# Two transformer blocks in one kernel: the joints between stages rearranged, conditioning rows on the ring's queue, a reordered last mixer

## The reference

```python
# first block; cs = silu(c)
for l in range(2):
    mod = cs @ ada_w[l] + ada_b[l]                       # 1024 x 6144
    sh1, sc1, g1, sh2, sc2, g2 = split(mod, 6)
    h = rms_norm(x, norm_mix_g[l]) * (1 + sc1) + sh1
    x = x + g1 * hybrid_mixer(h, w_in[l], w_out[l], ...)  # attention and retention
    h = rms_norm(x, norm_ffn_g[l]) * (1 + sc2) + sh2
    f = swiglu(h, ...) if l == 0 else moe_ffn(h, ...)     # dense FFN, then 8 experts, top 2
    x = x + g2 * f
x = rms_norm(x, final_norm_g)
# second block
for l in range(2):
    x = x + 0.5 * swiglu(rmsnorm(x, ffn1_norm[l]), ...)
    x = x + even_mixer(x) if l == 0 else x + odd_mixer(x)
    x = x + 0.5 * swiglu(rmsnorm(x, ffn2_norm[l]), ...)
```

## Time and profile before

| | |
|---|---|
| median of 3 runs | 2357.81 us (2356.74 to 2358.11) |
| profiled execution | 2357.99 us, span 2356.4 us |
| TensorE busy | 2257.9 us, 96% |
| VectorE busy | 1703.7 us, 72% |
| ScalarE busy | 1401.6 us, 59% |
| mean granted TensorE clock | 0.983 of full speed |
| moved by DMA | 571.54 MB, mean 243 GB/s |

### The profile page before, as it was taken

The page is one execution under the profiler, slowest core; times in us unless marked ns, Lnnn a source line. Parts: engine busy times, 40 slices in busy tenths (PEclk is TensorE's granted clock), DMA queues, the critical chain, the costliest instruction groups (busy, mean ns, idle before and its releaser), DMA issues.

```text
span 2356.4 us, 34524 instructions
## 1 busy us (share of the span) xinstructions
PE 2257.9 (96%) x10548; PEld 1865.6 (79%) x10548; DVE 1703.7 (72%) x2237; ACT 1401.6 (59%) x2059; POOL 27.8 (1%) x56
## 2 busy tenths in 40 slices
PE   7998998998999999999999899999999999879999
PEld 6877886787888888888887678877888888767887
DVE  5877777867989989999999855576555554754554
ACT  4545445556787787777777644465544544575443
POOL 0000110000000000000000000000000000000000
PEclk9999999998999999999999999999999999989999
DMA  9775885847999999999999765543656555412661
GB/s 374 271 223 193 306 296 177 303 137 205 362 349 367 352 349 367 348 367 355 355 360 351 269 196 180 195 152 118 199 183 194 171 184 172 151 45 68 210 196 54
DMA packets 403943, 571.54 MB, mean 243 GB/s; under 512 B 27868, under 2 KB 324376, under 8 KB 403832
## 3 DMA queue, kind: packets, MB, share of 16 engines
q1 hardware_dynamic: 394032, 543.13, 68.8%
q0 software_dynamic: 6304, 22.62, 3.0%
q10 hardware_dynamic: 3496, 4.39, 0.5%
HBM read 568.99 MB, written 1.05 MB: 242 GB/s over the span
## 4 chain that ended last, share of the span: by engine, by line
PE 84%; DVE 8%; ACT 5%; issue 3%; DMA 0%; ACTq 0%; DVEq 0%
PE bank L371 75%; DVE lo L350 3%; ACT hi L348 1%; PE bank L566 1%; PE bank L2668 1%; ACT xn L102 1%; DVE acc_sum L312 1%; PE bank L831 1%; PE bank L2795 1%; DVE small L102 1%; ACT aT_hi L102 1%; PE bank L2737 0%; PE bank L1862 0%; DVE rope_tmp L102 0%; DVE aT_lo L102 0%
## 5 line engine op out<-in xcount | busy, mean ns | idle before, releaser
L350 DVE TENSOR_TENSOR lo<-raw,hi 128x1024 fp32r<-128x1024 f32 x981 | 1158.8, 1222 | 180.8 <-ACT hi L348 167.1
L348 ACT ACTIVATE hi<-raw 128x1024 fp32r<-128x1024 f32 x981 | 987.7, 1054 | 95.6 <-PE bank L371 94.9
L371 PE MATMUL bank<-hi,aT_hi 128*128 128x512 f32 (+1 forms) x2016 | 812.7, 403 | 21.3 <-DVE aT_lo L102 8.5
L371 PE MATMUL bank<-hi,aT_lo 128*128 128x512 f32 (+1 forms) x2016 | 790.5, 392 | 0.0
L371 PE MATMUL bank<-lo,aT_hi 128*128 128x512 f32 (+1 forms) x2016 | 788.6, 391 | 0.0
L371 PEld LDWEIGHTS bank<-hi,aT_hi 128*128 128x128 f32 x2016 | 382.9, 190 | 104.3 <-issue 13.5
L371 PEld LDWEIGHTS bank<-hi,aT_lo 128*128 128x128 f32 x2016 | 381.7, 189 | 81.6
L371 PEld LDWEIGHTS bank<-lo,aT_hi 128*128 128x128 f32 x2016 | 383.2, 190 | 74.6 <-issue 1.7
L371 PE MATMUL bank<-hi,hidT_hi 128*128 128x512 f32 x792 | 310.1, 392 | 0.9 <-DVE hidT_lo L2676 0.9
L371 PE MATMUL bank<-hi,hidT_lo 128*128 128x512 f32 x792 | 308.4, 389 | 0.0
L371 PE MATMUL bank<-lo,hidT_hi 128*128 128x512 f32 x792 | 308.3, 389 | 0.0
(11 more groups left out here) (313 smaller groups left out, 1540.5 us busy)
## 6 DMA issues: line engine op xcount, KB each, us to landing
raw<-moe_w_gate SPq DMA_DIRECT2D x352, 256.0 KB
raw<-moe_w_up SPq DMA_DIRECT2D x352, 256.0 KB
raw<-moe_w_down SPq DMA_DIRECT2D x176, 512.0 KB
raw<-ffn_w_gu SPq DMA_DIRECT2D x352, 256.0 KB
raw<-ffn_w_down SPq DMA_DIRECT2D x110, 512.0 KB
raw<-ada_units SPq DMA_DIRECT2D x56, 512.0 KB
raw<-w_in SPq DMA_DIRECT2D x56, 512.0 KB
ada_slot<-ada_units POOLq DMA_DIRECT2D x40, 512.0 KB, 5.2
```

Source lines behind the costliest of these rows:

```text
L348: act.activation(hi[u % SPL][:, :], raw[r % RAW][:, :], ACTF.Copy).then_inc(hi_done, 1)
L350: dve.tensor_tensor(lo[u % SPL][:, :], raw[r % RAW][:, :], hi[u % SPL][:, :].bitcast(F32), ALU.subtract).then_inc(lo_done, 1)
L371: ins = pe.matmul(bank, left[a], right[b], start=first and n == 0, stop=last and n == 2)
```

## The change

1. **Start.** `fetch` can issue on SP; vectors, identity and biases of layer 0 go out there, ahead of the ring's first unit. Three direct units instead of four (`i < 3`). The four conditioning slabs are closed and added by their own functions, `close_slab` on TensorE and `add_slab` on VectorE, at separate places of the order.
2. **Layer 1's conditioning.** Bias columns, gates and columns move from the last step to `second_bias` and `second_conditioning` one and two steps earlier; slab (1, 9) becomes the last, half of it is summed in mixer 1's slots 4 and 5, and its columns are made in slot 7 by `last_ada_columns`.
3. **Starts of stages.** `modulated_first` makes each low part before the late additions; tile 1's root is computed in one pass (`rstd_whole`); in the dense FFN `turn_second` comes after the fourth unit instead of the second.
4. **Hybrid mixers.** The turn of attention's halves moves from slot 24, banks 2 and 3, to the end of slot 25, banks 6 and 7.
5. **Experts.** The second low part of the rows and the expert weights change places with the first one-hot products; these begin with tile 0's terms.
6. **First FFN of block 2.** The squares for the two norms are reordered; the rotary tables and lambda sums of the even mixer are made after its first products (`behind`), likewise the odd mixer's tables in the FFN before it.
7. **Odd mixer.** Rotation of the queries in slots 4 and 5, turn of the queries in slot 10, codes in banks 1 and 3, turn of the codes before the first scores, the copy of `probsT` on VectorE for heads 0 to 7, and the projections each one or two heads earlier.

```diff
-FFN_SLABS = [(0, 10)] + [(1, n) for n in (0, 1, 2, 3, 6, 7, 8, 9)] + [(0, 11)]
+FFN_SLABS = [(0, 10)] + [(1, n) for n in (0, 1, 2, 3, 6, 7, 8)] + [(0, 11), (1, 9)]
@@ acc_one
-        if i < 4 and j == 1:
+        if i < 3 and j == 1:
             direct_unit(i, r)
...
+        if j == 3 and i < 4:
+            cond_summed[i] = m
...
+    def close_slab(i):
+        PE.need(cond_summed[i], *bank_mark[2])
+        for b in range(4):
+            ins = pe.matmul(psum[2][:, 4 * i + b:4 * i + b + 1], acc_sum[i % 2][:, b * P:(b + 1) * P], ones_sq[:, 0:1],
+                            start=True, stop=True)
...
+    def add_slab(i):
+        c0 = col_of_slab(i)
+        part = (mod_cols if i < 3 else bias_cols)[:, c0:c0 + 4]
+        m = DVE.run([cond_columns[i], *bias_mark], dve.tensor_tensor, mod_cols[:, c0:c0 + 4], psum[2][:, 4 * i:4 * i + 4], part, ALU.add)
@@ pe_gate_up
-            if t == 0 and j == 1:
-                turn_second(turned)
...
+            if t == 0 and turned and j == turned.get("at", 1):
+                turn_second(turned)
@@ ffn_steps
         run_late()
+        behind()
...
         def at_end():
-            begin(STEPS - 1, 0, 1)
-            end(STEPS - 1)
             look_ahead(UNITS_D)
@@ set-up
-    vectors_in = fetch("vectors_in", (), (vec_rows[0:c_at + KD, :], io["vectors"]), (ident, io["tables"][:, 0:P]))
+    vectors_in = fetch("vectors_in", (), (vec_rows[0:c_at + KD, :], io["vectors"]), (ident, io["tables"][:, 0:P]), Q=SP)
@@ modulated_first
         h = hi_pair(0, 2, a)
+        run_late(1)
+        done += lo_pair(0, 2, h)
         split_to(st["use"] + 3)
         a = full_pair(0, full_act, 0, turned[2], 4, gain, bias, marks)
-        done += lo_pair(0, 2, h)
         h = hi_pair(0, 4, a)
-        run_late(1)
+        done += lo_pair(0, 4, h)
+        run_late()
         split_to(st["use"] + 4)
-        run_late()
         a = full_pair(0, full_act, 0, turned[3], 6, gain, bias, marks)
-        done += lo_pair(0, 4, h)
@@ first_conditioning
+        fetch_bias(0, (), SP)
         load_acc()
-        fetch_bias(0, ())
...
         acc_to(14)
         aT_marks = [[m for i in range(2) for m in lo_pair(t, 2 * i, his[t][i])] for t in range(NT)]
-        close_accs(3, 2)
+        add_slab(2)
         acc_to(16)
-        close_accs(4, 2)
+        close_slab(3)
         split_to(1)
-        ready = modulated_gain(0, 0, range(4, 8), bank_mark[2][0])
+        ready = modulated_gain(0, 0, range(4, 8), add_slab(3))
@@ conditioning of layer 1
+    def last_ada_columns():
+        n = STEPS - 2
...
+        m = DVE.run([m], dve.tensor_tensor, mod_cols[:, 28:32], psum[5][:, 0:4], bias_cols[:, 28:32], ALU.add)
...
+    def second_conditioning():
+        dve.wait_ge(ada_rows, STEPS - 2)
+        m = DVE.run(bias_mark, dve.tensor_tensor, mod_cols[:, 0:28], ada_cols[:, 0:28], bias_cols[:, 0:28], ALU.add)
+        DVE.need(gates_in[0])
+        gates_mark[:] = [DVE.did(dve.tensor_tensor(gates[:, 1, :], gates[:, 1, :], mod_rows[:, 0:D], ALU.add))]
@@ slot of the hybrid mixer
+            if n in (4, 5) and layer:
+                ada_sums(STEPS - 2, 0, 1, (2 * n - 4, 2 * n - 3))
+            if n == 7 and layer:
+                last_ada_columns()
...
-                oaT_marks.extend(turn_half(lambda t, k: xn[:, t, k * P:(k + 1) * P], (2, 3), o_a,
-                                           lambda k: col("att_out_g", 4 * layer + k), oaT))
...
+            if n == 25:
+                oaT_marks.extend(turn_half(lambda t, k: xn[:, t, k * P:(k + 1) * P], (6, 7), o_a,
+                                           lambda k: col("att_out_g", 4 * layer + k), oaT))
@@ free_heads, turn
+            if i < 8:
+                dve.wait_ge(turned_heads, i + 1)
+                if i >= 2:
+                    dve.wait_ge(valued, i - 1)
+                dve.tensor_copy(probsT[:, i % 2, :], psum[b][:, :]).then_inc(kept, 1)
@@ rest
-            PE.need(busy)
-            pe.reg_load(most[mybir.EngineType.PE], busiest_i[0:1, 0:1])
-            first_pair()
+            first_hi[:] = [parts[1]]
+            split_lo(1)
+            route["weights"] = weights(eq4, w4, out, e, ready)
+            first_pair(lambda: (PE.need(busy), pe.reg_load(most[mybir.EngineType.PE], busiest_i[0:1, 0:1])))
             split_to(st["use"] + 6)
-            route["weights"] = weights(eq4, w4, out, e, ready)
@@ normed_final, second
             groups = turn(1, 0) + turn(1, 1)
-            gained(0)
+            g0 = gained(0)
             done = plain_tile(1, groups, gain)
-            a = gained(1)
+            g1 = gained(1)
+            a = square(0, xg, ss, [g0, sq])
+            b = square(1, x, pp, [x_mark[1]])
+            a = square(1, xg, ss, [g1, b])
@@ odd_mixer
-                     ahead=lambda j: first_heads(8 + j))
+        slab_by_unit(GQ, evacuate("codes", lambda t: proj[:, t, CQ:GQ]), (1, 3), lambda j: slot(8 + j),
...
         turn(0)
+        code_rstd()
         scores(2)
-        turn_codes()
+        rotate_kpe()
+        project_ukv()
         values(0)
         turn(1)
         scores(3)
-        code_squares()
-        rotate_kpe()
+        whole_k(0)
+        project_uq(0)
```

More of the change, by code:

```diff
@@ L987, in dense_ffn @@
         scale = (lambda t: r_keep[:, t:t + 1]) if g is None else None
-        marks = ffn_steps(turned, scale=scale, final=final, aside=aside, dense=True)
+        marks = ffn_steps(turned, scale=scale, final=final, aside=aside, dense=True, behind=behind)
         for half in range(2):
@@ L1034, in ada_sums @@
             dve.wait_ge(ada_rows, n + i)
-        for k in range(half * KD // 2, (half + 1) * KD // 2):
+        for k in ks or range(half * KD // 2, (half + 1) * KD // 2):
             j, kk = k // 2, k % 2
@@ L1882, in free_heads, with odd_tables, gained, gain_row @@
         return scores, turn, values, finish
+    def odd_tables():
+        free = table("decay")
+        def gained(at, angles, gain, width, parts):
+            d = width // (2 * parts)
+            g = gain.rearrange("p (a z d) -> p a z d", a=parts, z=2)
+            views = {}
+            for i, name in enumerate(angles):
+                for z in range(2):
+                    n = NT * parts * d
+                    v = free[:, at + (2 * i + z) * n:at + (2 * i + z + 1) * n].rearrange("p (t a d) -> p t a d", t=NT, a=parts)
+                    x = table(name).rearrange("p (t a d) -> p t a d", t=NT, a=parts)
+                    views[i, z] = v
+                    prepared["tables"] = DVE.run([], dve.tensor_tensor, v, x, g[:, :, z, :].unsqueeze(1).to_broadcast([P, NT, parts, d]), ALU.mult)
+            return views
+        def gain_row():
+            v = free[:, 768:864]
+            prepared["gain"] = [v, DVE.run([], dve.tensor_tensor, v[:, 0:64], row("od_mla_q_norm_2")[:, 0:64], row("od_mla_k_norm_2")[:, 0:64],
+                                    ALU.mult), DVE.run([], dve.memset, v[:, 64:96], 1.0)]
+        prepared["gq"] = gained(0, ("gqa_cos", "gqa_sin"), row("od_gqa_q_norm_2"), 64, 2)
+        prepared["gk"] = gained(256, ("gqa_cos", "gqa_sin"), row("od_gqa_k_norm_2"), 64, 2)
+        prepared["mq"] = gained(512, ("mla_cos", "mla_sin"), row("od_mla_q_norm_2")[:, 64:96], 32, 1)
+        prepared["mk"] = gained(640, ("mla_cos", "mla_sin"), row("od_mla_k_norm_2")[:, 64:96], 32, 1)
+        gain_row()
     def odd_mixer():
@@ L1895, in odd_mixer @@
         m, c = {}, {}
-        free = table("decay")
+        gq_tabs, gk_tabs, mq_tabs, mk_tabs = (prepared[n] for n in ("gq", "gk", "mq", "mk"))
+        c.update(tables=prepared["tables"], gain=prepared["gain"])
         kf = k_full[:, :, :].rearrange("p t (n d) -> p t n d", n=8)
@@ L1908, in evacuate @@
             return out_of_bank
-        def gained(at, angles, gain, width, parts):
-            d = width // (2 * parts)
-            g = gain.rearrange("p (a z d) -> p a z d", a=parts, z=2)
-            views = {}
-            for i, name in enumerate(angles):
-                for z in range(2):
-                    n = NT * parts * d
-                    v = free[:, at + (2 * i + z) * n:at + (2 * i + z + 1) * n].rearrange("p (t a d) -> p t a d", t=NT, a=parts)
-                    x = table(name).rearrange("p (t a d) -> p t a d", t=NT, a=parts)
-                    views[i, z] = v
-                    c["tables"] = DVE.run([], dve.tensor_tensor, v, x, g[:, :, z, :].unsqueeze(1).to_broadcast([P, NT, parts, d]), ALU.mult)
-            return views
         def rotate(x1, x2, tabs, tmp, out1, out2, marks):
@@ L2904, in end @@
         def end(n, i=0):
[L2905 to L2906 removed]
+            if n == STEPS - 3:
+                second_bias()
+            elif n == STEPS - 2:
+                PE.need(*bias_mark)
+                ada_out(n - 1)
+                second_conditioning()
             elif n > 0:
```

248 lines of the change are left out of this document (132 added, 116 removed).

## The result

2331.61 us, the median of four runs (2327.37 to 2333.91), against 2357.96 (2356.74 to 2358.37): a ratio of 0.9893, 95% interval 0.9881 to 0.9905. Forecast: 2330.6. The profiled execution took 2333.91 with a span of 2332.3, so its sum has to make 24.1 us, not the 26.4 of the medians. That the total is within 1.0 us is luck: three terms are wrong by 1.8 to 2.8 us each, of both signs.

The account below looks back on a forecast made before the run. TensorE was taken to bound the kernel, busy 2257.9 of 2356.4 us, with idle time and lower clock at the joints between stages. Eight gains, A to H, sum to 27.4 us: 2357.99 - 27.4 = 2330.6 us, range 2315 to 2344.

Parts of the forecast that it names:

- A: First conditioning: rows issued ahead of the ring and one direct unit fewer bring the first mixer product earlier; 4.6 us won.
- rival 1: First conditioning: the rows land no earlier, only the shorter TensorE list counts, A is 2.6, total 2332.6; chance 0.10.
- B: Attention halves turned one slot later in both mixers: 0 in mixer 0, 1.2 us won in mixer 1.
- C: Start of the dense FFN: all four units of tile 0 go before tile 1's turn; 2.5 us won.
- D: Layer 1's conditioning: work moved from the FFN's end, less the price of slab (1, 9) in mixer 1; 2.0 us won.
- F: First FFN of block 2: reordered squares remove waits of 1.60 and 4.07; 5.6 us won.
- G: Tables of the even mixer: four operations leave a full VectorE queue; 0.9 us won.
- E: Start of the experts: second low part behind the one-hots, weights moved from before VectorE's branch; 2.1 us won.
- H: Odd mixer: 1.5 us won up to turn(0), 7 more from there to scores(8); 8.5 us won.
- rival 4: Odd mixer: copies stand behind VectorE's queue, 4 us a head, the stage loses 32, total 2369.6; chance 0.03.
- Rival 3: Fewer pauses keep 2.4 GHz; half the 56 us at 1.2 GHz goes, 12.6 us more, total 2318; chance 0.13.
- the three joints: Three places between stages with mean granted clock shares 0.84, 0.79 and 0.88, holding 56 us at 1.2 GHz.

Follow-up runs that it names:

- rows_act: The changed kernel with first vectors, identity and biases issued on ScalarE's queue again, beside the ring's units on SyncE's; 2332.95 us.
- thin_sums: The changed kernel with the four sums of slab (1, 9) in mixer 1 made over 4 columns instead of 512; 2327.49 us.
- copies_36: The changed kernel with only the odd mixer's copies of heads 3 and 6 back on ScalarE; 2333.04 us.
- lo_first: The changed kernel with the second low part of the routed rows ahead of the one-hots again; 2331.23 us.
- count_first: The changed kernel with TensorE's register load of the busiest count ahead of the gathering products again; 2335.23 us.

## Why the prediction was right, and where it was not

**A, 1.8 for 4.6: rival 1 in substance.** The step that failed is "the first ring unit is issued 1.7 us later for the four copies ahead", costed at no more than that. It is issued 1.9 later, but VectorE got it only at 8.64 us, and TensorE's first direct unit starts at 9.91, later than the 8.22 before. So the third direct unit ends at 28.06, not near 25.7, and the last close at 39.11, not 37.1. What is left of A at the first product is 2.7, and rows_act has 2.6 of it without moving the rows. This is the size that rival 1 gave to the shorter TensorE list alone; the list and the new order of closes and low part were not run apart. Then 0.9 more goes while the first products still come 0.43 us apart (0.23 later on), and this part differs between executions: 0.1 in thin_sums, 1.4 in copies_36. The rule that I had weighed against this term, the Trainium skill's "Issuing engines are not separate DMA queues" (DMA: Bandwidth & Descriptors), that copies of all issuers interleave on the same 16 DMA engines, is compatible with the two runs and not tested by them. The identity is used at 5.02 with the rows ahead of the ring and at 7.31 beside it, the first product moved 0.12, but rows_act changes the queue and the order of issue together.

**B, C, D, F, G: 12.4 for 12.2.** The sum is closer than it can be known to be, by the spreads in the table. C's tile 1 starts at 191.88 behind a wait of 2.36; the walk's 194.4, less the lead of 2.0, had it at 192.4 behind 3.8. D's turn came 4.5 earlier than the FFN's end asks, as said; its price was right in size (2.1 for 2.3) and wrong in place: at the turn of slot 8, not before the router's fold, whose wait fell from 1.11 to 0.72. F's walk held: no wait between the tiles and one of 1.23 before the second step (0.9 forecast).

**E, 3.9 for 2.1.** The failed step is that "after the branch its next operation comes 3.87 later, whatever stands there". VectorE had 2.99 there now, and TensorE's last wait fell from 3.48 to 2.50. I also left out that the register load no longer stands in front of the gathering (2.30 to 0.32), though alone it is worth 0.4. And the low part's earlier place, 1.1 of my 2.1, is worth 0.4 alone in lo_first, so most of the gain is elsewhere; that it is the weights' place is not shown.

**H, 6.0 for 8.5.** The start was nearly right: 2.6 for 1.5 up to turn(0), with no wait for the bank and 5.24 for the keys (4.7 forecast). From turn(0) to scores(8) it was 45.0 instead of 41. The failed step is "the eight copies of 0.60 that go to VectorE leave ScalarE 33": relief of an engine that was not full was counted as a gain (ScalarE was busy 34.10 of these 48.20 us before, and not the 37.9 of my count), and the queue that the copies moved into was looked at only in rival 4, at 0.03. That mechanism is real; it took about 3 (2.5 to 4.0) in the stretch, not 32, since only three of the eight copies show a wait behind them. And of the 3.2 us that this stretch did win, 2.9 is TensorE's busy time (36.10 to 33.20) and 0.3 idle time (12.1 to 11.8): the waits that I expected to shrink are together as long as before.

**Rival 3**, the clock, happened in part: of the 24.1 us, about 6 are busy time of products that both kernels have, and the time at 1.2 GHz fell from 79 to 63 us, where the rival asked for 28 less. Its reading that each low stretch of the three joints begins behind a wait of 2 us or more misses two in the trace of before: the one from 536.4 begins within products of 8 columns behind a wait of 0.16, the one from 2140.6 behind a wait of 0.69.

## What to carry to other kernels

Before an operation is moved to the engine with more idle time, read what will stand in front of it there at that moment; a chain with a root on a third engine holds every later entry of the queue until the root is there. When a wait was taken away here, the next one was three times close behind it and took its place: the bank of the codes, bank 3 in mixer 1 and the early keys won 0 of 3.5, 1.5 and 2 us. And a total that fits says little of its terms; the lead, stage by stage, says more, once several profiles of the same work show how far it moves by itself.

## What the runs showed of the hardware

The same wait is followed by a different clock in different executions. At the dense FFN's start all kernels with C wait 2.36 in front of tile 1, but the granted clock over the next products was 1.00 in the changed kernel and 0.83 in copies_36 and count_first, which did not touch that stage:

```profile
186.00:206.00 20.00, 16.85 (x77) 12.82 (x78) 12.61 (x22) 12.59 (x22) 0.00 (x0) 1.00 0.50 154
```

```profile
186.00:206.00 20.00, 16.48 (x61) 12.22 (x62) 12.61 (x20) 12.02 (x20) 0.00 (x0) 0.83 0.47 151
```

The lead across C was 2.9 to 3.0 in ten of the thirteen profiles, 1.4 in one and under 0.1 in these two. It is not the only such place: across E, F and H, too, kernels that do the same work differ by 2 to 4 us (last column of the table). This can account for the 6.5 us by which the four runs of the changed kernel differ, but only one of the four was profiled. The kernel before is no steadier: its four runs here differ by 1.6, the seven beside the last experiments by 6.8 (2351.69 to 2358.47). Why the clock falls after one such wait and not after another, the runs do not show.
